# Rows of an expert group taken straight from x, and an eleventh weight slot filled in the mixer

## The reference, cut to what matters

```python
# one layer of the second block; the kernel counts the layers l = 0, 1
x = x + gate2 * token_mixer(modulate(rms_norm(x, g1), shift0, scale1), ...)
h = modulate(rms_norm(x, g2), shift3, scale4)
x = x + gate5 * hier_moe(h, ...)

def rms_norm(x, g):
    return x * lax.rsqrt(jnp.mean(x * x, axis=-1, keepdims=True) + 1e-6) * g

def hier_moe(h, w_grp, b_grp, w_exp, b_exp, w1, w3, w2):
    # each row picks 1 of 4 groups, then 2 of the group's 8 experts
    # expert: (silu(h @ w1) * (h @ w3)) @ w2, summed with the router's weights
```

## Time and profile before

| what | value |
| --- | --- |
| time, three runs | 2291.93, 2291.80, 2289.04 us; median 2291.8 us |
| profiled execution (given by its span, first to last instruction) | 2292.1 us |
| TensorE busy | 2260.4 us, 99% of the span |
| VectorE, ScalarE, GpSimd busy | 1050.4, 463.2, 73.8 us |
| bytes moved by DMA | 671.70 MB, 293 GB/s on average |
| chain that ended last | PE 88%, DMA 9%, DVE 2% of the span |
| mean granted TensorE clock | 0.994 of full speed |
| expert stage of layer 0 on PE | from 1097 to 1551 us |
| expert stage of layer 1 on PE | from 1832 to 2285 us |

### The profile page before, as it was taken

How to read it: one execution, slowest core, us unless ns; L and a number is a source line. 1 busy time by engine, 2 the same in 40 slices (tenths; PEclk the granted TensorE clock), 3 DMA queues, 4 the chain that set the end, 5 groups by cost and what they waited for, 6 DMA issues and landing times.

```text
span 2292.1 us, 26684 instructions
## 1 busy us (share of the span) xinstructions
PE 2260.4 (99%) x11270; PEld 1373.6 (60%) x11270; DVE 1050.4 (46%) x2056; ACT 463.2 (20%) x1037; POOL 73.8 (3%) x130
## 2 busy tenths in 40 slices
PE   9999999999999999999999999999999999999998
PEld 6569548886497459997443333335999643333342
DVE  3578756667588557675211111125767411111122
ACT  2411003357111011220211111101122121111111
POOL 2000000000100000000000000000000000000000
PEclk9999999999999999999999999999999999999999
DMA  7278725345689424237999999994423899999997
GB/s 294 110 305 363 313 77 199 149 184 184 241 360 388 163 87 177 97 148 299 406 428 427 428 427 428 427 418 179 169 89 120 368 420 428 427 427 427 429 426 286
DMA packets 59171, 671.70 MB, mean 293 GB/s; under 512 B 7504, under 2 KB 7792, under 8 KB 18720
## 3 DMA queue, kind: packets, MB, share of 16 engines
q1 hardware_dynamic: 51888, 649.45, 68.9%
q0 software_dynamic: 7152, 20.43, 2.7%
HBM read 666.59 MB, written 3.26 MB: 292 GB/s over the span
## 4 chain that ended last, share of the span: by engine, by line
PE 88%; DMA 9%; DVE 2%; issue 0%; ACT 0%; SPq 0%; POOL 0%; DVEq 0%; POOLq 0%; ACTq 0%
PE ps L101 85%; DMA ring<-in_exp_w 5%; DMA arena<-in_exp_w 3%; PE ps L349 1%; DVE arena L117 1%; DMA arena<-ssm_rows 1%; PE ps L2979 1%; DVE arena L114 0%; PE ps L638 0%; DMA ring<-in_attn_w_in 0%; PE ps L2129 0%; DVE X L117 0%; PE ps L1327 0%; ACT arena L106 0%; PE ps L2954 0%
## 5 line engine op out<-in xcount | busy, mean ns | idle before, releaser
L101 PE MATMUL ps<-arena 128*128 128x128 f32 (+8 forms) x4484 | 1011.9, 448 | 14.1 <-DMA arena<-in_exp_w 5.8
L101 PEld LDWEIGHTS ps<-arena 128*128 128x128 f32 (+2 forms) x4484 | 513.7, 170 | 467.4 <-issue 437.7
L101 PE MATMUL ps<-ring,arena 128*64 128x512 f32 (+2 forms) x1720 | 460.7, 584 | 1.6 <-DMA ring<-in_exp_w 1.6
L101 PE MATMUL ps<-XTGB,ring 128*128 128x256 f32 (+1 forms) x2032 | 382.5, 344 | 0.0
L101 PEld LDWEIGHTS ps<-XTGB,ring 128*128 128x128 f32 x2032 | 333.5, 191 | 43.8 <-issue 9.9
L101 PEld LDWEIGHTS ps<-ring,arena 128*64 128x64 f32 (+1 forms) x1720 | 173.8, 150 | 259.6 <-issue 255.0
L122 DVE COPY arena<-ps 128x512 f32<-128x512 f32 (+5 forms) x133 | 63.3, 496 | 407.0 <-PE ps L101 288.1
L121 ACT COPY arena<-ps 128x512 f32<-128x512 f32 (+3 forms) x187 | 84.8, 472 | 696.7 <-PE ps L2979 286.5
L101 PE MATMUL ps<-XTGB,arena 128*128 128x128 f32 (+2 forms) x768 | 192.3, 404 | 0.0
L117 DVE TENSOR_TENSOR arena<-ps,arena 128x256 f32<-128x256 f32 (+5 forms) x290 | 127.0, 475 | 117.6 <-PE ps L101 88.0
L101 PE MATMUL ps<-ring,XTGB 128*128 128x512 f32 (+3 forms) x484 | 168.4, 503 | 2.6 <-DMA ring<-in_attn_w_in 2.5
(11 more groups left out here) (154 smaller groups left out, 1004.9 us busy)
## 6 DMA issues: line engine op xcount, KB each, us to landing
arena<-in_exp_w SPq DMA_DIRECT2D x90, 2048.0 KB, 27.4
ring<-in_exp_w SPq DMA_DIRECT2D x68, 2048.0 KB, 28.0
ring<-in_mlp_w SPq DMA_DIRECT2D x25, 2048.0 KB, 11.6
ring<-in_ada_w SPq DMA_DIRECT2D x20, 2048.0 KB, 9.7
XTGB<-in_exp_w SPq DMA_DIRECT2D x18, 2048.0 KB, 32.2
ring<-in_ssm_w_in SPq DMA_DIRECT2D x12, 2048.0 KB, 7.4
ring<-in_w_in SPq DMA_DIRECT2D x12, 2048.0 KB, 7.8
ring<-in_gate_w SPq DMA_DIRECT2D x12, 2048.0 KB, 8.1
```

The source lines that it names most:

```text
L101: return self.e.matmul(o, lhsT=lhsT, rhs=rhs, start=start, stop=stop, skip_group_check=True)
```

## The change

The scaled rows `H2` are no longer written. The selector takes the scale instead: `pgs` is `pg` times `rs2`, row by row, and `group_rows` multiplies `pgs` with X itself. The new column order is taken by the gather: it reads its stationary side from `xr` with a step of eight elements (`xr_q[:, :, c]`), and so each gather waits for both halves of `xr`. `group_rows` for groups 2 and 3 waits for earlier sums into X.

The 4096 elements at the arena's start, where the retention mask `dmask`, `f_F` and free space now lie together, become an eleventh slot (number 10). `mix_sp` loads the first slab of the expert stage, w1 of expert 0, into it right after the three branch weights, as soon as the mask and `f_F` have been read for the last time. The mask is overwritten, so POOL loads it again (768 KB) for layer 1. `rw` moves elsewhere, `x_s` and `x_h` share one buffer, and everything behind the first area moves up by 512 elements. The path for overfull experts (`general`), which is not taken here, gets its own scaling.

```diff
         ring = Places(slots + [None, None, XTGB] + [arena.ap[:, TOP + j * SLAB:TOP + (j + 1) * SLAB] for j in range(3)]
+                      + [arena.ap[:, 0:SLAB]])
...
         def mlp1_pool(pool):
-            for name in ("cm", "dmask"):
-                pool.landed(pool.e.dma_start(C[name], d["const_" + name]), "late", "late")
+            pool.landed(pool.e.dma_start(C["cm"], d["const_cm"]), "late", "late")
+            pool.landed(pool.e.dma_start(C["dmask"], d["const_dmask"]), "dmask", ("dmask", 0))
...
         def mix_sp(sp, l):
+            ring.tenant[NRING + 6] = ("early", l)
+            ring.turn.insert(0, NRING + 6)
+            slab(sp, ("exp_w1", l, 0, 0), "exp_w1", l * NE * P * SLAB, 8, 512, hold=True)
...
         def mix_act(act, l, nn):
-            square_act(act, nn + 1, 0, H2, X, at("rows", nn + 1, 0))
+            act.wait_ge(at("rows", nn + 1, 0))
+            k = act.then_inc(act.act(sq_out, X[:, 0, :], ACT.Square, acc=rs2[:, 0:1]), ("sq", nn + 1, 0))
...
-            rms_rows(act, nn + 1, 1, H2, X)
...
         def mix_dve(v, l, nn):
-            v.wait_ge(at("late"))
+            v.wait_ge(at("dmask", l))
...
                     rms_var(v, nn + 1, 0)
-                    rms_rows(v, nn + 1, 0, H2, X)
...
         def mix_pool(pool, l, nn):
+                pool.wait_ge(at("free", last_over_mask[0]))
+                pool.landed(pool.e.dma_start(C["dmask"], d["const_dmask"]), "dmask", ("dmask", 1))
...
         def moe_sp(sp, l):
+            ring.turn.append(NRING + 6)
...
                         for key, off in zip(keys, offs):
-                            slab(sp, key, nm, off, kc, n)
+                            if key == ("exp_w1", l, 0, 0):
+                                continue
+                            if ring.tenant[ring.turn[0]] in HALVED[l]:
+                                load_behind_halves(sp, [key], nm, [off], kc, n)
+                            else:
+                                slab(sp, key, nm, off, kc, n)
...
             def group_rows(g, n, between=None):
-                pe.wait_ge(at("pg", l, g), at("hh", nn - 1, 1, 0), at("hh", nn - 1, 1, 4))
+                pe.wait_ge(at("pgs", l, g), at("rows", nn - 1, 0), at("rows", nn - 1, 1))
+                if g >= 2:
+                    pe.wait_ge(*[at("sum", l, g - 2, t, n) for t in range(2)])
...
-                    ins = pe.mm(ps, pg[:, t, :], H2[:, t, n * 512:(n + 1) * 512], t == 0, t == 1)
+                    ins = pe.mm(ps, pgs[:, t, :], X[:, t, n * 512:(n + 1) * 512], t == 0, t == 1)
...
             def gather(i, c0):
-                pe.wait_ge(at("psel", l, i), at("xr ready", l, i // 4, c0 // 4))
+                pe.wait_ge(at("psel", l, i), at("xr ready", l, i // 4, 0), at("xr ready", l, i // 4, 1))
...
-                    ins = pe.mm(ps[:, (c - c0) * P:(c - c0 + 1) * P], xr[:, c * P:(c + 1) * P], psel, True, True)
+                    ins = pe.mm(ps[:, (c - c0) * P:(c - c0 + 1) * P], xr_q[:, :, c], psel, True, True)
...
                 act.wait_ge(at("exp_w1", l, i))
                 if i >= 1:
-                    act.wait_ge(at("xh", l, i - 1))
+                    act.wait_ge(at("xht", l, i - 1))
...
             def group_places(g):
-                v.wait_ge(at("gcode", l))
+                v.wait_ge(at("gcode", l), at("rstd", nn - 1, 0), at("rstd", nn - 1, 1))
                 if g:
-                    v.wait_ge(at("xr", l, g - 1, 1), at("pgt", l, g - 1),
+                    v.wait_ge(at("xr", l, g - 1, 1))
+                for t in range(2):
+                    v.then_inc(v.ts(pgs[:, t, :], C["iota"], gcode[:, t, g:g + 1], rs2[:, t:t + 1], ALU.is_equal, ALU.mult),
+                               ("pgs", l, g))
+                if g:
+                    v.wait_ge(at("pgt", l, g - 1),
```

More of the change, by code:

```diff
@@ L220, in build @@
         for name in ("x0", "x1", "aq0", "aq1", "aq2", "aq3", "ident", "rope", "consts", "c", "pos", "gb", "sink", "maska", "ssmp", "late", "keep", "half0", "half1", "half2", "half3", "ada_b", "cols", "mod", "gate_b",
-                     "fox_fb", "mla_g", "abias", "router_b", "rw", "srow", "se0", "se1", "se2", "out"):
+                     "fox_fb", "mla_g", "abias", "router_b", "rw", "dmask", "srow", "se0", "se1", "se2", "out"):
             sems[name] = ctx.enter_context(nc.semaphore("s_" + name))
-        for i in range(NRING + 6):
+        for i in range(NRING + 7):
             sems[f"ring{i}"] = ctx.enter_context(nc.semaphore(f"s_ring{i}"))
@@ L234, in build @@
             sems[f"gen{l}_x"] = ctx.enter_context(nc.semaphore(f"s_gen{l}_x"))
-        ring = Places(slots + [None, None, XTGB] + [arena.ap[:, TOP + j * SLAB:TOP + (j + 1) * SLAB] for j in range(3)])
+        ring = Places(slots + [None, None, XTGB] + [arena.ap[:, TOP + j * SLAB:TOP + (j + 1) * SLAB] for j in range(3)]
+                      + [arena.ap[:, 0:SLAB]])
         ring.begin(NRING)
@@ L1629, in build @@
         arena.pos = 0
+        C["dmask"] = arena.get(consts["dmask"])
+        f_at = arena.pos
+        arena.pos = SLAB
         for name in LATE:
-            C[name] = arena.get(consts[name])
+            if name != "dmask":
+                C[name] = arena.get(consts[name])
         ctab, stab = C["rope2c"], C["rope2s"]
         posf = small[:, 40:42]
-        MOD = arena.get(3, D)
-        GATE = {2: arena.ap[:, ASZ - D:ASZ], 5: MOD[:, 2, :]}
+        GATE = {2: arena.ap[:, ASZ - D:ASZ], 5: arena.get(D)}
         gb = arena.get(24)
@@ L1792, in build @@
         lf, fbb = arena.get(2, 4), arena.get(4)
-        f_F = [MOD[:, 0:2, :].rearrange("p a f -> p (a f)")[:, 384 * i:384 * (i + 1)] for i in range(4)]
-        rw = MOD[:, 1, 512:800].rearrange("p (c e) -> p c e", c=8)
+        f_F = [arena.ap[:, f_at + 384 * i:f_at + 384 * (i + 1)] for i in range(4)]
+        assert f_at + 4 * 384 <= SLAB
         rwg = XTGB[:, 2048:2336].rearrange("p (c e) -> p c e", c=8)
@@ L1826, in build @@
         bS4 = arena.get(4, T)
+        rw = arena.get(8, 36)
         assert arena.pos <= ASZ - D
@@ L2254, in fox_scores @@
                 pe.mm(ps[:, P:T], C["ones"], F[:, 0:P], False, False)
-                pe.then_inc(pe.mm(ps[:, P:384], LE, F[:, P:384], False, True), ("cs", 1, l, h))
+                pe.then_inc(pe.mm(ps[:, P:384], LE, F[:, P:384], False, True), ("cs", 1, l, h),
+                            *([("free", ("early", l))] if h == 3 else []))
             for i in range(6):
@@ L2467, in mix_act @@
             for n in range(2):
-                act.wait_ge(at("rows half", nn + 1, 1, n))
-                act.then_inc(act.act(H2[:, 1, n * 512:(n + 1) * 512], X[:, 1, n * 512:(n + 1) * 512], ACT.Square, scale=1.0 / 32,
+                act.wait_ge(at("rows half", nn + 1, 1, n), k)
+                act.then_inc(act.act(sq_out[:, n * 512:(n + 1) * 512], X[:, 1, n * 512:(n + 1) * 512], ACT.Square, scale=1.0 / 32,
                                      acc=small[:, 171:172] if n else rs2[:, 1:2]), ("sq", nn + 1, 1))
-            rms_rows(act, nn + 1, 1, H2, X)
         def mix_dve(v, l, nn):
@@ L2517, in mix_dve @@
                 v.then_inc(v.tt(r_s[h % 2], ps_of("rs", l, h)[:, 0:384], C["dmask"][:, h * 384:(h + 1) * 384], ALU.mult),
-                           ("rsm", l, h), ("read", "rs", l, h))
+                           ("rsm", l, h), ("read", "rs", l, h), *([("free", ("early", l))] if h == 3 else []))
                 if h:
@@ L2559, in mix_dve @@
             lfk = v.then_inc(v.stt(lf, lf, 0.0, lt_, ALU.min, ALU.subtract))
-            v.wait_ge(lfk, at("consts"))
+            v.wait_ge(lfk, at("consts"), at("free", last_over_mask[0]) if l else None)
             for i in range(4):
@@ L2722, in build @@
         m1, sel = arena.get(2, 8), arena.get(2, 8)
-        pg = arena.get(2, P)
+        pg, pgs = arena.get(2, P), arena.get(2, P)
         pgt = arena.get(T)
@@ L2754, in build @@
         g_s = x_s.rearrange("p (a b) -> p a b", a=2)
-        g_u = x_h.rearrange("p (a b) -> p a b", a=2)
+        g_u = x_ht.rearrange("p a b -> p (a b)").rearrange("p (a b) -> p a b", a=2)
+        g_n = slots[3][:, 2 * D:4 * D].rearrange("p (t f) -> p t f", t=2)
         g_y = slots[3][:, 0:2 * D].rearrange("p (t f) -> p t f", t=2)
@@ L2772, in general_pe @@
             w1v, w3v, w2v = general_views()
+            pe.wait_ge(at("gen rows", l))
             for t in range(2):
                 for c in range(8):
-                    ins = pe.e.transpose(psb[2 * t + c // 4][:, c % 4 * P:(c % 4 + 1) * P], H2[:, t, c * P:(c + 1) * P],
+                    ins = pe.e.transpose(psb[2 * t + c // 4][:, c % 4 * P:(c % 4 + 1) * P], g_n[:, t, c:D:8],
                                          C["ident"])
@@ L2801, in general_act @@
         def general_act(act, l):
+            act.wait_ge(at("gen x", l))
+            for t in range(2):
+                act.then_inc(act.act(g_n[:, t, :], X[:, t, :], ACT.Copy, scale=rs2[:, t:t + 1]), ("gen rows", l))
             act.wait_ge(at("gen xt", l))
```

18 lines of the change are left out of this document (10 added, 8 removed).

## The result

The kernel after takes 2339.4 us (median of 5 runs, 2335.39 to 2343.33) against 2291.8 us: a ratio of 1.021, with a 95% interval of 1.0198 to 1.0221. It is 47.6 us slower, where 2281 us, 11 us faster, had been forecast.

The account below looks back on a forecast made before the run. The prediction took slab landings to bound PE in the expert stages; gains of 6.7 us in layer 0 and 4.6 in layer 1, mixers 0, made 11.3 us off 2291.8: 2281 us, range 2276.5 to 2287.

Parts of the forecast that it names:

- the strided gather: Expert-stage gathers, 256 stationary loads a layer at step eight: taken as 0 us, at most 12.8 us a layer.
- three signs of being wrong: Slower gathers of a pair, DMA share below 0.97 from 1110 to 1135 us, or a long wait at pairs 12 to 14.
- Rival (c): Strided gather becomes PE's bound and all landing waits vanish: 12.8 us slower, about 2305 us; chance 0.06.
- the rule weighed beside it: Trainium skill's SBUF page: 16-byte lines, a penalty for reads in a new line each time, steps up to four fp32 free.
- The slot: Eleventh slot in the expert stages: first slab loads free in the mixer's idle end, later slabs land 4.9 us earlier.
- the caps: Limits on how far a late pair's use moves up, 4.9 us plus its margin: 6.7 us layer 0, 5.0 layer 1.
- Rival (b): DMA engines run dry near 1110 us and the lead is lost: gain 1 to 5 us, about 2289; chance 0.09.
- The final gain's load: POOL's 512 KB load in layer 1 starts some 15 us earlier, delaying pair 15's w1 by 1.2 us.
- The start of the stage: PE's path at each expert stage's start: 0.8 us waiting for both xr halves, 0.1 for pgs, 0.9 a layer.
- the 14.6 us that a longer lead could give back: PE time lost to slab waits and half clock behind them: 7.64 us in layer 0, 6.91 in layer 1.
- Half clock (a): Smaller gain, 5 to 8.5 us: half-clock stretches of 1.7 us each at stage start or pair 15, about 2284; chance 0.14.
- The rest at no cost: group_rows' waits, ACT's transpose wait, the mask's second load and rw's load behind it: 0 us.

Follow-up runs that it names:

- the last version: Kernel after with ACT's copy of xr reordering (step in the read), slab halves loaded two by two and the final gain's load at the end: 2281.65 us.
- the kernels with the couples: Kernel after, reordering in ACT's copy, slabs 12 to 15 in halves two by two: 2284.88 us; with the final gain's load at the end too: 2283.08 us.

## Why the prediction was wrong

**The step that failed** is the one on the strided gather: "So I take 0; the upper bound is the whole 50 ns for each load". It took a product's cost from rows of another kind of instruction and put it at nothing. The measured price is 30.7 us / 256 = 120 ns of PE time for a load, 61.4 us in both layers, in place of 0. Rows 5 and 6 were rows of transposes, and of these they are true. A gather is a product. One sign stood in the profile of before: a gather's load at step one already took 192 ns (the group's mean above), where a transpose's takes 140, so the two were not the same operation. Their overlap would not have told it: 192 ns at a spacing of 0.12 us and a transpose's 190 ns at 0.13 look alike, and only the first kind grew. "Gather loads take near 240 ns and their pace stays at 0.11 us a load" was wrong on both: 335 ns and 0.243 us (and the pace before was 0.12, not 0.11). Of its three signs of being wrong two came: the gathers took longer, and the DMA share from 1110 to 1135 us was 0.91, below 0.97. The third, a long wait at pairs 12 to 14, did not come in the kernel after.

**The upper bound was no bound.** It was taken from one difference in one kind of instruction (190 - 140 ns). The products with the identity show the same data at the same step with 333 ns. Why the step slows a product's loads (by 143 ns, and the pace with them) and a transpose's by 50 ns and no pace, no run here tells; that cause stays open.

**Rival (c) had the mechanism and not the size.** Its own sum with the measured price is 61.4 + 1.8 - 14.6 = 48.6 us slower; 47.6 was measured on the medians (45.9 between the two profiled executions). So what it says of the rest (all landing waits vanish) was right, as the windows show. It had a chance of 0.06, although the rule weighed beside it spoke for it.

**The slot.** That the first slab is loaded into idle time and costs nothing was right: in the kernel after it lands 12.5 us after its issue, as the DMA view from 1000 to 1013 us shows (KB, us to landing), long before its use at 1106 us.

```profile
arena<-in_exp_w SPq DMA_DIRECT2D x1, 2048.0 KB, 12.5
```

What the slot brings was too high: 8.6 us measured, where the caps made 11.3 + 1.8 = 13.1; and the rest of the change costs 8.6 - 5.9 = 2.7 us, where the sum had 1.8. The profile of the kernel with the reordering in the copy shows where 4.9 of the missing 11.3 - 5.9 = 5.4 us are: it waits 5.1 us for slabs, where the sum left 1.4, and its two starts cost 3.0 us, where the sum had 1.8.

(1) The waits. The sum moved every landing by a whole place, but pair 12's w1 is still late, by 0.74 us in layer 0 and 1.62 in layer 1, so the slabs come less than a place earlier. Rival (b)'s mechanism took part of the lead: the transfers run short before the halves are released. The windows from 1090 to 1152 us of the kernel before, the one with the reordering in the copy, and the one with the copy written in runs:

```profile
1090.00:1152.00 62.00, 61.00 (x296) 27.85 (x296) 14.13 (x54) 16.20 (x35) 1.83 (x3) 0.97 0.99 407
```

```profile
1090.00:1152.00 62.00, 59.66 (x290) 27.15 (x290) 14.68 (x56) 14.84 (x34) 1.83 (x3) 0.97 0.98 393
```

```profile
1090.00:1152.00 62.00, 60.09 (x297) 27.33 (x297) 14.64 (x56) 14.40 (x36) 1.83 (x3) 1.00 1.00 404
```

At 393 instead of 407 GB/s 0.87 MB less are moved in 62 us, which is 2.0 us of transfer; at 404 it is 0.4 us (estimates from these rows). The last two kernels issue the same loads in the same order. In the first of them PE starts the stage at half clock (0.50 from 1098 to 1100 us) and the halves are released 15.6 us after the issue into XTGB, in the second 13.7 us after it. So the half clock at the start, which the prediction took to be mostly absorbed by the caps, costs part of the lead too; how much of the time this is, no run sets apart.

(2) The final gain's load was foreseen, with its place and its wait "of about 1 us": 1.05 us were seen, and they are in the sum.

(3) The start of the stage costs more than 0.9 us. Both stretches at full clock: PE from the group selection's last small product to pair 0's w1, in layer 1 of the kernel before

```profile
1832.51 0.36 PE L101 MATMUL ps<-arena,c_tri 128*128 128x4 f32 x2
...
1839.95 2.37 PE L101 MATMUL ps<-ring,arena 128*64 128x512 f32 x10
```

and in layer 0 of the last version

```profile
1095.58 0.36 PE L101 MATMUL ps<-arena,c_tri 128*128 128x4 f32 x2
...
1096.84 1.98 PE L101 MATMUL ps<-X,arena 128*128 128x512 f32 x4 [0.90 <-DVE arena L111]
...
1102.16 2.60 PE L101 MATMUL ps<-arena 128*128 128x128 f32 x17 [0.72 <-DVE arena L117]
1104.12 0.64 PE L101 MATMUL ps<-ring,arena 128*64 128x512 f32 x1
```

are 7.44 and 8.54 us: 1.1 us, and with the slower copy 0.4 more. Of the 1.1, `pgs` is 0.18 (PE waits 0.90 us for it, 0.72 for `pg` before) where the prediction took 0.1, and the rest comes with the wait of 0.72 us before the gathers.

**The basis.** The prediction set the span of the profiled execution (2292.1 us) beside the median time (2291.8) as if they were one measure. In the runs on record a time is about 1.8 us longer than its span (2339.84 and 2338.0 in the kernel after), so that execution took about 2293.9 us, 2.1 above the median. Its mean clock of 0.994 is low: of 59 other executions of this kernel two have 0.994, the others more. So the 14.6 us that a longer lead could give back were read from a slow execution. The last version's figures come near them all the same: 8.3 us gained, 2.2 paid at the starts and 2.7 of waits left are 13.2.

**Half clock (a).** That it left the last pairs was right. At the starts it comes and goes between executions of the same instructions (layer 0 of the kernels with the couples: 0.79 and 1.00 from 1096 to 1104 us), and four products of `group_rows` take 3.53 us with it and 1.98 without. Between the layers it is not new: with the reordering in the copy the granted clock is 0.57 from 1547 to 1554 us, but the kernel before has 0.86 from 1552 to 1564 us as well. No experiment set these stretches apart.

**The rest at no cost** holds as far as the profiles show: with the gathers at step one, no wait for the mask, `rw` or the sums stands among PE's waits, and the waits for slabs are down to those of pairs 12 to 15.

## What to carry to other kernels

In these runs the stationary side of a 128x128 fp32 product could be read at step one or two almost for free; from step three on the loads came further apart, and where products follow each other without pause that is PE's pace. A reordering belongs where data is copied anyway, with the step on the side where it is free (here ACT's read of PSUM). And a cost is bounded only by rows of the same kind of instruction: a transpose's load says little of a product's, and a bound taken across kinds is a guess that wants a wide range.

## What the runs showed that was not expected

- Stationary loads of 128x128 fp32 in products: recorded as 192 ns at step one, 335 at step eight; for 256 loads 31.7, 33.2, 46.8, 61.1 and 62.3 us of PE time at steps one, two, three, four and eight. In transposes step eight costs 50 ns that no pace shows. A transpose's load at step one among products at step eight is recorded with 269 ns in place of 143.
- ACT's copy of 128x512 from PSUM: 0.59 us in order and with a read at step eight, 1.02 us with a write at a step of 512 bytes.
- A kernel that is bound by landings can hide a large cost's true size: 61.4 us more of PE work made the kernel 47.6 us slower, as the waits and the half clock behind them (14.6 us in the profile before) went with it.
